# Last SSD group's output blocks and the layer norm behind them in token halves

## The chip, the cores and the metric

The kernel runs on one core of one Trainium2 chip. Its time is the device time of one launch in microseconds (us). Before the change it is 3307.63 us, the median of 3 runs (3304.9 to 3308.18).

## The reference

The program computes five layers on one sequence of 1024 tokens and width 1024, all in float32: an RG-LRU and latent-attention layer, a state space layer (SSD), and then a block of a feed-forward layer (FFN), a mixer and a second FFN. The change is in the seam between the SSD layer and the first FFN:

```
def _ssd_layer(x, w_in, conv_w, conv_b, dt_bias, a_log, d_skip, norm_w, w_out):
    ...
    y = _ssd_scan(xs, dt, a_neg, bm, cm) + d_skip.astype(jnp.float32)[:, None] * xs.astype(jnp.float32)
    y = y.reshape(bsz, seqlen, SSD_INNER) * jax.nn.silu(z.astype(jnp.float32))
    yg = y.reshape(bsz, seqlen, SSD_GROUPS, SSD_INNER // SSD_GROUPS)
    yg = yg * lax.rsqrt(jnp.mean(yg * yg, axis=-1, keepdims=True) + 1e-6)
    y = (yg.reshape(bsz, seqlen, SSD_INNER) * norm_w.astype(jnp.float32)).astype(x.dtype)
    return jnp.einsum('bse,ed->bsd', y, w_out)
...
            x = _layernorm(DN_ALPHA * x + y, ssd_ln_g[j], ssd_ln_b[j])
...
        h = rms_norm(x, ffn1_pre_g[l])
        x = x + 0.5 * rms_norm(swiglu(h, ffn1_w_in[l], ffn1_w_out[l]), ffn1_post_g[l])
```

There are four SSD groups of 512 channels. Each group is gated, normed by the root mean square over its 512 channels, and multiplied by its 512 rows of `w_out`.

## The kernel before

Activations lie transposed, features on the 128 partitions and tokens along the free axis: `ACC` is [128, 8 tiles, 1024 tokens]. A "token half" is 512 tokens, `half(0)` or `half(1)`, and h0 and h1 below. Each engine has a program of its own, written out in the order in which it runs, and semaphores join them. Nothing reorders them: an instruction that waits holds up all behind it on its engine.

A float32 product is made of three fast ones (fp32r). Weights `WS` and inputs are split into a high part (by ScalarE, `split_hi`, L333) and a low part (by VectorE, `split_lo`, L340), and TensorE adds high x high, high x low and low x high (`block_products`, L376). A block is 128 output features; in the SSD output projection it has 4 contraction tiles, so 12 products in one token half and 24 in both, and in the FFN 8 tiles, so 24 products in one half. Weight blocks alternate between two slots, and so do the PSUM banks `PS[0]` and `PS[1]`. Sums over features, which the norms want, are matmuls with `ONES` in plain float32; here each shows as two records in the trace.

The last SSD group (`g` = 3) runs so. The scan goes over 8 chunks of 128 tokens. In chunk 7 TensorE does the first two output blocks on h0 (`ssd_last_half`) between the chunk's first product and `ssd_outputs`. Their input `YLH`, `YLL` needs the gate's last block `z3`, its silu, the gating by VectorE (`ssd_last_gate`) and the split (`high`, `ssd_last_low`). Behind the scan come, on TensorE: 8 sums of squares (L1777), the first two blocks on h1, six blocks on both halves, 4 filler matmuls (`keep_busy`, L357), then the layer norm: 2 row sums (L1503) and 16 sums of squares (L1507). VectorE multiplies each block's PSUM by the group's root and adds it to `ACC` (`acc_vector`, L1461 and L1462), and adds rows up for the mean (L1472). The layer norm centres `ACC` (L1488), ScalarE squares it (L1511) and takes the root with Ln and Exp (L1516, L1517), VectorE scales (L1494), ScalarE adds the bias (L1521).

The first FFN begins with 8 blocks on h0 and 8 on h1 (j = 0 to 7 each; `ffn_tensor`). Its input is `ACC` again split (`pre_high` L2186, `pre_low` L2195) and squared for its own norm (L2190); GpSimd adds these squares up (`pre_sum`, L2203) for h0, TensorE for h1 (`head_row`, L2214). `pre_rows` (L2207) and `pre_rstd` (L2220, L2224) give the root that `ffn_hidden` (L2712 to L2721) needs before it can free a PSUM bank. The next two weight blocks are split in `ffn_gated` (L2635), behind the silu. After block 1 of h0 TensorE runs 15 filler matmuls.

Of the kernel before, what the change touches and what calls it, by code (L numbers as in the profile page):

```python
# [20 lines left out]
P = 128  # L21
# [123 lines left out]
def _build(nc, ctx, ins, out):  # L145
# [63 lines left out]
    YLH = at("YLH", 64, [P, 4, SEQ], F32R)  # L209
    YLL = at("YLL", 80, [P, 4, SEQ], F32R)  # L210
# [1243 lines left out]
    def acc_vector(dve, st, b0, turn, rooted=0):  # L1454

        for m in range(KT):
            b = b0 + m
            dve.wait_ge(BLOCK_DONE[b % 2], times(b))
            if rooted:
                dve.wait_ge(RSTD, rooted)  # L1460
                st.link(nc.vector.tensor_tensor(PS[b % 2][:], PS[b % 2][:], T[1][:], ALU.mult))  # L1461
            nc.vector.tensor_tensor(ACC[:, m], ACC[:, m], PS[b % 2][:], ALU.add).then_inc(PS_READ[b % 2], 1)  # L1462
            if m == KT - 1:
                row_sum(dve, st, b, m, turn)
            split_lo(dve, b + 2, cols=cols_of(b + 2))
            if 0 < m < KT - 1:
                row_sum(dve, st, b, m, turn)
# [30 lines left out]
    def ln_tensor(pe, turn, name):
        sq0 = NORM[name][1]
        keep_busy(PA, 4)  # L1500
        pe.wait_ge(LN_VECTOR, LN_TURN * turn + MSUM + 1)
        for h in range(2):
            nc.tensor.matmul(PB[:, half(h)], ONES[:], T[2][:, half(h)], start=True, stop=True).then_inc(MROW, 1)  # L1503
        for h in range(2):
            for k in range(KT):
                pe.wait_ge(SQ, sq0 + KT * h + k + 1)
                nc.tensor.matmul(PA[:, half(h)], ONES[:], SQB[:, k, half(h)], start=(k == 0), stop=(k == KT - 1)).then_inc(SUMMED, 1)  # L1507
# [387 lines left out]
    def ssd_last_scalar(act, st, g):  # L1895
# [19 lines left out]
        for k in range(4):  # L1915
            high(0, k)
# [1906 lines left out]
```

## Time and profile before

| | |
|---|---|
| median of 3 runs | 3307.63 us |
| profiled execution: its span, first to last instruction (the page gives no other time of it) | 3306.2 us |
| TensorE busy | 3189.7 us, 96% |
| VectorE busy | 2013.8 us, 61% |
| ScalarE busy | 1287.6 us, 39% |
| GpSimd busy | 356.9 us, 11% |
| mean granted TensorE clock | 0.990 |

Of the chain that ended last, 83% of the span is TensorE's. So a change counts where TensorE stands still or does what need not be done. The stage of the change lies at 1270 to 1430 us of the span. A timeline row reads: start, duration, engine, line, operation, output<-inputs, count, and in brackets how long the engine was idle before it and who ended that. Matmuls overlap, so a matmul's duration is longer than the distance from one start to the next.

### The profile page before, as it was taken

How to read it: one execution, taken by the hardware profiler on the slowest of the kernel's cores; microseconds unless marked ns; L12 is line 12 of the kernel's file. 1: busy time of each engine (PE TensorE's matmuls, PEld its weight loads, DVE VectorE, ACT ScalarE, POOL GpSimd, SP SyncE). 2: the span in 40 equal slices, each digit the busy share in tenths (PEclk: the TensorE clock that was granted, in tenths of full speed). 3: DMA queues.
4: the chain of work that ended last, by engine and by line, in shares of the span. 5: the costliest groups of instructions: out<-in, count | busy, mean ns of one | idle time of the engine just before them, and what ended most of it. 6: DMA issues, size and time to landing. Idle time of an engine off the chain costs nothing.

```text
span 3306.2 us, 40063 instructions
## 1 busy us (share of the span) xinstructions
PE 3189.7 (96%) x15986; PEld 2491.6 (75%) x15986; DVE 2013.8 (61%) x2760; ACT 1287.6 (39%) x1906; POOL 356.9 (11%) x421
## 2 busy tenths in 40 slices
PE   8999999999999998899999999998988899999999
PEld 7765577878787786578888888786666678888887
DVE  5544567664554645667777665586664877767334
ACT  2554435452525344643333223413525542323123
POOL 1011000110302011100000003140011200000012
PEclk9999999999999999899999999999999999999999
DMA  6220111222513132332223334423044432224234
GB/s 161 50 42 6 55 52 53 76 88 77 103 52 118 48 92 68 99 105 90 77 90 111 128 112 134 140 74 90 1 115 127 146 118 77 77 102 161 75 100 136
DMA packets 359543, 299.54 MB, mean 91 GB/s; under 512 B 55200, under 2 KB 320768, under 8 KB 358816
## 3 DMA queue, kind: packets, MB, share of 16 engines
q1 hardware_dynamic: 336496, 215.29, 22.3%
q0 software_dynamic: 22864, 81.69, 8.0%
q8 instruction: 128, 2.10, 0.3%
q14 instruction: 55, 0.45, 0.0%
HBM read 240.45 MB, written 52.95 MB: 89 GB/s over the span
## 4 chain that ended last, share of the span: by engine, by line
PE 83%; DVE 8%; ACT 4%; issue 3%; DMA 1%; SPq 0%; POOL 0%; DVEq 0%; ACTq 0%; POOLq 0%
PE PS L376 48%; PE PS L2529 13%; PE PA L2529 7%; PE PA L904 1%; PE PS L893 1%; PE PS L1100 1%; PE PB L916 1%; DVE WL L340 1%; PE PB L1840 1%; PE PS L1105 1%; PE PA L416 1%; PE PB L1179 1%; PE PB L1846 1%; PE PA L1822 1%; PE PS L1553 1%
## 5 line engine op out<-in xcount | busy, mean ns | idle before, releaser
L376 PE MATMUL PS<-XH,WH 128*128 128x512 f32 x1744 | 594.0, 405 | 25.7 <-DVE XL L2195 15.4
L333 ACT ACTIVATE WH<-WS 128x1024 fp32r<-128x1024 f32 (+1 forms) x251 | 242.3, 968 | 836.4 <-PE PS L376 811.5
L376 PE MATMUL PS<-XH,WL 128*128 128x512 f32 x1680 | 553.5, 391 | 0.0
L376 PE MATMUL PS<-XL,WH 128*128 128x512 f32 x1648 | 541.5, 391 | 0.0
L376 PEld LDWEIGHTS PS<-XH,WH 128*128 128x128 f32 x1744 | 326.0, 188 | 120.1 <-issue 21.4
L340 DVE TENSOR_TENSOR WL<-WS,WH 128x1024 fp32r<-128x1024 f32 (+1 forms) x251 | 283.0, 1128 | 155.2 <-ACT WH L333 141.4
L376 PEld LDWEIGHTS PS<-XH,WL 128*128 128x128 f32 x1680 | 316.4, 188 | 67.6
L376 PEld LDWEIGHTS PS<-XL,WH 128*128 128x128 f32 x1648 | 310.5, 188 | 68.0 <-issue 4.1
L376 PE MATMUL PS<-TQH,WH 128*128 128x512 f32 x448 | 160.1, 392 | 1.4 <-DVE WL L340 1.4
L376 PE MATMUL PS<-TQH,WL 128*128 128x512 f32 x448 | 158.8, 389 | 0.0
L376 PE MATMUL PS<-TQL,WH 128*128 128x512 f32 x448 | 158.7, 389 | 0.0
L2529 PE MATMUL PS<-XH,PH 128*128 128x512 f32 x360 | 140.2, 390 | 1.7 <-issue 1.7
L2529 PE MATMUL PS<-XH,PL 128*128 128x512 f32 x360 | 140.1, 389 | 0.0
L2529 PE MATMUL PS<-XL,PH 128*128 128x512 f32 x360 | 140.0, 389 | 0.0
L1953 ACT ACTIVATE DEC<-DEC,NCS 128x128 f32<-128x128 f32 x256 | 78.3, 388 | 99.1 <-POOL DEC L2069 99.0
L1974 DVE TENSOR_TENSOR DEC<-DEC,PB 128x1024 f32<-128x1024 f32 x32 | 39.1, 1221 | 125.3 <-ACT DEC L1953 103.5
L2529 PE MATMUL PS<-TQH,PH 128*128 128x512 f32 x288 | 112.5, 391 | 1.7 <-DVE U3S L2772 1.0
L2529 PE MATMUL PS<-TQH,PL 128*128 128x512 f32 x288 | 112.1, 389 | 0.0
L2529 PE MATMUL PS<-TQL,PH 128*128 128x512 f32 x288 | 112.0, 389 | 0.0
L2529 PE MATMUL PA<-TQH,PH 128*128 128x512 f32 x288 | 112.0, 389 | 0.0
L2529 PE MATMUL PA<-TQL,PH 128*128 128x512 f32 x288 | 112.0, 389 | 0.0
L2529 PE MATMUL PA<-TQH,PL 128*128 128x512 f32 x288 | 112.0, 389 | 0.0
(697 smaller groups left out, 6164.3 us busy)
## 6 DMA issues: line engine op xcount, KB each, us to landing
RAW<-in_ffn_w_in_dram SPq DMA_DIRECT2D x36, 1024.0 KB, 5.5
WS<-in_ffn_w_out_dram SPq DMA_DIRECT2D x48, 512.0 KB, 3.9
WS<-in_ssd_w_in_dram SPq DMA_DIRECT2D x40, 512.0 KB, 3.8
DEC<-ssd_decay_sums SPq DMA_DIRECT2D x32, 512.0 KB, 4.8
WS<-in_ffn_w_in_dram SPq DMA_DIRECT2D x32, 512.0 KB, 4.1
CDX<-ssd_decays SPq DMA_DIRECT2D x56, 256.0 KB, 3.7
TQF<-ffn_hidden POOLq DMA_DIRECT2D x14, 1024.0 KB, 8.3
x_residual<-ACC POOLq DMA_DIRECT2D x6, 2048.0 KB, 7.9
```

The lines of the kernel that those rows point to most:

```text
L333: nc.scalar.activation(WH[:, s, 0:cols], WS[:, s, 0:cols], ACT.Copy).then_inc(W_HI[s], 1)
L340: nc.vector.tensor_tensor(WL[:, s, 0:cols], WS[:, s, 0:cols], WH[:, s, 0:cols].bitcast(F32), ALU.subtract).then_inc(W_LO[s], 1)
L376: last = nc.tensor.matmul(PS[s][0:width, c], w[:, s, k * width:(k + 1) * width], x[:, k - x0, c], start=(k == 0 and j == 0), stop=(k == kt ...
L416: last = nc.tensor.matmul(PA[:, h * HALF:(h + 1) * HALF], ONES[:], bufs[k % 2][:, h * HALF:(h + 1) * HALF], start=(k == 0), stop=(k == kts ...
L893: last = nc.tensor.matmul(PS[s][:, a + c * P:a + (c + m) * P], self.queries(p, s)[:, qb * P:(qb + 1) * P], self.keys(p, s)[:, c * P:(c + m ...
L904: last = nc.tensor.transpose(PA[:, s * HALF + (kb - 4 * c) * P:s * HALF + (kb - 4 * c + 1) * P], self.probs(u, s)[:, kb * P:(kb + 1) * P], ...
L916: last = nc.tensor.matmul(PB[HD * s:HD * s + HD, HALF + (qb % 4) * P:HALF + (qb % 4 + 1) * P], self.values(p, s, kb), PT[u % 2][:, s, kb * ...
L1100: nc.tensor.matmul(PS[s][:, a + c * P:a + (c + m) * P], QT[t][rows, 0, q], KTT[t][rows, 0, c * P:(c + m) * P], start=True, stop=False)
L1105: last = nc.tensor.matmul(PS[s][:, a + c * P:a + (c + m) * P], QT[t][rows, 1, q], KTT[0][rows, 1, c * P:(c + m) * P], start=False, stop=True)
L1953: last = nc.scalar.activation(d, d, ACT.Exp, bias=NCS[:, c, k:k + 1])
L1974: v.tensor_tensor(DEC[n % 2][:], DEC[n % 2][:], PB[:, 0:P].unsqueeze(1).broadcast_to([P, HPG, P]), ALU.mult).then_inc(SMR, 1)
L2529: last = nc.tensor.matmul(bank, w[:, j, k * P:(k + 1) * P], x[:, k], start=(j in (A11, S2, S1) and k == 0 and t == 0), stop=(k == 3 and t ...
```

## The change

- The output weights of the last group are split once, into the free h1 halves of `XH` and `XL` (`out_high`, `out_low`), and serve both halves. The eight blocks run on h0 first and then on h1, each in half a bank (`out_bank`), so four products can stand before the first is read.
- The split of the first two weights, the gate's silu and the gated input come ahead of the decay of chunk 7 on ScalarE (`ssd_last_scalar`), and on VectorE ahead of that chunk's mixing. The third output weight's load stands later in SyncE's queue.
- The squares of the group's norm are added on GpSimd (`ssd_last_added`), and TensorE sums once for each half. Rows for the mean are added on GpSimd too (`ln2_row`).
- The layer norm of h0 runs beside the h1 output blocks, and that of h1 beside the FFN's h0 blocks (`ln2_beside_scalar`, `ln2_beside_vector`, `ln2_beside_tensor`). The FFN's squares of h1 are added on GpSimd as well. Both fillers are gone.

```diff
@@ ssd_sync
-                if c % 2 == 0:
+                if c % 2 == 0 and (c < TT - 2 or g < LAST):
                     ssd_load(sp, *after[c // 2 - 1])
@@ TensorE
+    def ssd_out_half(pe, h, m):
+        b = SSD_AT[LAST, "out", m]
+        s, n = b % 2, KT * h + m
+        if h == 0:
+            pe.wait_ge(W_LO[s], times(b))
+            if m < 2:
+                pe.wait_ge(PS_READ[s], times(b) - 1)
+        if 4 <= n < 12:
+            pe.wait_ge(OUT_FREE, OUT_FREE0 + n - 3)
+        if n >= 12:
+            pe.wait_ge(PS_READ[s], times(b - 4))
...
+    def ssd_last_out(pe):
         for m in range(2, KT):
-            block_products(pe, SSD_AT[g, "out", m], YLH, YLL, kt=4)
+            ssd_out_half(pe, 0, m)
+            if m == 2:
+                ssd_last_sum(pe, 0)
+            if m == 6:
+                ssd_last_sum(pe, 1)
+        for m in range(KT):
+            ssd_out_half(pe, 1, m)
+            if m == 0:
+                ln2_mean(pe, 0)
+            if m == 2:
+                ln2_squares(pe, 0)
...
-                    pe.wait_ge(RSTD, NORM["ln2"][0] + 2)
-                    keep_busy(PA, 15)
...
+    def ln2_beside_tensor(pe, j):
+        if j == 0:
+            ln2_mean(pe, 1)
+        if j == 2:
+            ln2_squares(pe, 1)
+        if j == 7:
+            pre_rows(pe, 0, 1)
@@ ScalarE
+        weights(0)
+        high(0, 0)
+        high(0, 1)
+        ssd_gate_silu(act, g, 3)
+        high(0, 2)
+        high(0, 3)
+        weights(1)
+        ssd_decay(act, g, TT - 1)
         for k in range(4):
             square(0, k)
+        weights(2)
+        weights(3)
+        nc.scalar.activation(EP[:, 8:9], EP[:, 0:1], ACT.Ln)
+        high(1, 0)
+        high(1, 1)
+        weights(4)
+        root(0)
...
+    def ln2_scalar(act, st):
         for k in range(KT):
+            ln2_square(act, 0, k)
+        nc.scalar.activation(EP[:, 10:11], EP[:, 0:1], ACT.Ln)
+        ln2_rstd(act, st, 0)
+        for k in range(KT):
+            ln2_bias(act, 0, k)
+            pre_high(act, 0, 0, k)
+        for k in range(KT):
+            pre_square(act, 0, 0, k)
+        nc.scalar.activation(EP[:, 11:12], EP[:, 0:1], ACT.Ln)
+        pre_rstd(act, st, 0, 0)
+        for k in range(KT):
+            ln2_square(act, 1, k)
+
+    def ln2_beside_scalar(act, st, f):
+        if f == 0:
+            ln2_rstd(act, st, 1)
+        if f == 1:
+            for k in range(KT):
+                ln2_bias(act, 1, k)
+                pre_high(act, 0, 1, k)
+        if f == 2:
+            for k in range(KT):
+                pre_square(act, 0, 1, k)
+        if f == 3:
+            pre_rstd(act, st, 0, 1)
@@ VectorE
+        for m in range(4, KT):
+            ssd_out_read(dve, st, 0, m)
+        ssd_out_read(dve, st, 1, 0)
+        ln2_center(dve, 0, range(KT))
+        for m in (1, 2):
+            ssd_out_read(dve, st, 1, m)
+        for b in (B_FFN1, B_FFN1 + 1):
+            split_lo(dve, b)
+        ssd_out_read(dve, st, 1, 3)
+        ln2_apply(dve, 0, range(3))
+        ssd_out_read(dve, st, 1, 4)
+        for k in range(KT):
+            pre_low(dve, 0, 0, k)
+            if k + 3 < KT:
+                ln2_apply(dve, 0, [k + 3])
+            if k < 3:
+                ssd_out_read(dve, st, 1, 5 + k)
...
+    def ln2_beside_vector(dve, f):
+        if f == 1:
+            ln2_apply(dve, 1, range(KT))
+        if f == 2:
+            for k in range(KT):
+                pre_low(dve, 0, 1, k)
@@ GpSimd
     def ln2_pool(pool):
+        ssd_last_added(pool, 0)
+        for m in range(1, 3):
+            ln2_row(pool, 0, m)
+        ssd_last_added(pool, 1)
+        for m in range(3, KT):
+            ln2_row(pool, 0, m)
+        for m in range(1, KT):
+            ln2_row(pool, 1, m)
+        for h in range(2):
+            for k in range(KT):
+                pre_sum(pool, 0, h, k)
+            pool.wait_ge(LNB, (3 + h) * KT)
+            spill_pool(pool, 0, h)
```

`ssd_out_read` is the pair of VectorE instructions that multiplies half a bank by the root and adds it to `ACC`; `OUT_FREE` and `PS_READ` count them.

Two places show how the order moves. ScalarE in the FFN's h0 blocks, from the root of the FFN's norm (Ln, Exp) on. `T_67` is the gate's silu, `WH` a weight split, `SQQ` and `T_69` the squares of the FFN's norm. Before:

```order
L2224 ACTIVATE T_69<-T_69 128x512
L1521 ACTIVATE ACC<-ACC,VT 128x512 x8
L2635 ACT_TABLE_LOAD
L2635 ACTIVATE T_67<-T_67 128x512
L333 ACTIVATE WH<-WS 128x1024 x2
L2186 ACTIVATE XH<-ACC,VT 128x512
L2190 ACTIVATE T_69<-ACC 128x512
L2186 ACTIVATE XH<-ACC,VT 128x512
L2190 ACTIVATE SQQ_191<-ACC 128x512
L2635 ACTIVATE T_67<-T_67 128x512
L333 ACTIVATE WH<-WS 128x1024 x2
```

The same place now, up to the second silu:

```order
L2340 ACTIVATE T_69<-T_69 128x512
L1488 ACTIVATE SQB<-ACC 128x512 x8
L2808 ACT_TABLE_LOAD
L2808 ACTIVATE T_67<-T_67 128x512
L333 ACTIVATE WH<-WS 128x1024 x2
L1498 ACT_TABLE_LOAD
L1498 ACTIVATE ZT<-PA,EP 128x512
L1499 ACT_TABLE_LOAD
L1499 ACTIVATE ZT<-ZT 128x512
L2808 ACT_TABLE_LOAD
L2808 ACTIVATE T_67<-T_67 128x512
L333 ACTIVATE WH<-WS 128x1024 x2
```

Where ScalarE had two splits and two squares between silus, it now has the layer norm's root; behind the second pair of `WH` come 8 pairs of bias (L1510) and high part (L2295), and behind the third 8 squares (L2306).

VectorE in the same blocks, third and fourth hidden tile (`T_67`, `T_68` from PSUM; `WL` the low part of a weight). Before, behind the fourth weight split of h0:

```order
L2195 SCALAR_TENSOR_TENSOR XL<-ACC,VT,XH 128x512 x4
L2712 TENSOR_TENSOR T_67<-PS,T_69 128x512
L340 TENSOR_TENSOR WL<-WS,WH 128x1024
L2718 TENSOR_TENSOR T_68<-PS,T_69 128x512
L2721 TENSOR_TENSOR T_68<-T_68,T_67 128x512
L340 TENSOR_TENSOR WL<-WS,WH 128x1024
L2195 SCALAR_TENSOR_TENSOR XL<-ACC,VT,XH 128x512 x2
```

Now:

```order
L1505 SCALAR_TENSOR_TENSOR ACC<-ACC,VT,ZT 128x512 x8
L2887 TENSOR_TENSOR T_67<-PS,T_69 128x512
L340 TENSOR_TENSOR WL<-WS,WH 128x1024
L2893 TENSOR_TENSOR T_68<-PS,T_69 128x512
L2896 TENSOR_TENSOR T_68<-T_68,T_67 128x512
L340 TENSOR_TENSOR WL<-WS,WH 128x1024
L2311 SCALAR_TENSOR_TENSOR XL<-ACC,VT,XH 128x512 x8
```

The low parts of h1, which were spread in twos and fours, stand in one run of 8 before the fourth hidden tile, and the layer norm's scaling of h1 in one run of 8 before the third.

## Rows read from the trace of the kernel before

**Rows 1.** TensorE's waits, 1225 to 1500 us: waiter <- releaser: total, times, longest
```profile
PE PS L376 <- DVE XL L2195: 7.9, 8, 2.2
PE PS L376 <- DVE YLL L2035: 7.6, 1, 7.6
```
**Rows 2.** Busy time by stretch (stretch, its length, engines, clock, DMA share, GB/s)
```profile
1269.91:1287.26 17.35, 9.75 (x56) 7.82 (x56) 7.56 (x11) 9.79 (x19) 1.15 (x2) 0.70 0.14 47
1287.26:1334.60 47.34, 45.84 (x187) 34.64 (x186) 34.58 (x36) 14.21 (x20) 0.00 (x0) 1.00 0.16 47
...
1356.00:1390.20 34.20, 25.60 (x80) 17.25 (x80) 20.51 (x23) 29.37 (x42) 11.83 (x9) 0.75 0.21 80
1390.20:1429.70 39.50, 39.49 (x159) 29.89 (x160) 18.65 (x23) 15.69 (x24) 0.00 (x0) 1.00 0.51 150
```
**Rows 3.** TensorE in order of time
```profile
1266.97 0.61 PE L376 MATMUL PS<-XH,WL 128*128 128x512 f32 x2
...
1277.51 0.77 PE L376 MATMUL PS<-YLH,WH 128*128 128x512 f32 x1 [7.61 <-DVE YLL L2035]
...
1282.29 0.39 PE L376 MATMUL PS<-YLH,WL 128*128 128x512 f32 x1
...
1285.37 1.09 PE L1840 MATMUL PB<-DEC,XTOK 128*64 128x128 f32 x16
...
1287.26 7.38 PE L1777 MATMUL PA<-T,ONES 128*128 128x512 f32 x16
...
1363.49 0.79 PE L376 MATMUL PS<-XH,WH 128*128 128x512 f32 x1 [2.23 <-DVE XL L2195]
...
1378.51 0.39 PE L376 MATMUL PS<-XL,WH 128*128 128x512 f32 x1
...
1382.39 6.63 PE L357 MATMUL PA<-ONES 128*128 128x256 f32 x30
```
**Rows 4.** ScalarE in order of time
```profile
1270.08 2.44 ACT L1953 ACTIVATE DEC<-DEC,NCS 128x128 f32<-128x128 f32 x8 [7.22 <-POOL DEC L2069]
1272.54 1.28 ACT L1877 ACT_TABLE_LOAD   x1
1273.84 1.02 ACT L1877 ACTIVATE ZT<-PS 128x1024 f32<-128x1024 f32 x1
...
1275.28 2.55 ACT L1902 ACTIVATE YLH<-ZT,VT 128x512 fp32r<-128x512 f32 x4
1277.73 2.18 ACT L1913 ACTIVATE T<-ZT 128x512 f32<-128x512 f32 x4
...
1355.46 0.71 ACT L1521 ACTIVATE ACC<-ACC,VT 128x512 f32<-128x512 f32 x1
1356.20 0.72 ACT L2186 ACTIVATE XH<-ACC,VT 128x512 fp32r<-128x512 f32 x1
1356.83 0.61 ACT L2190 ACTIVATE SQQ<-ACC 128x512 f32<-128x512 f32 x1
```
**Rows 5.** VectorE in order of time
```profile
1288.10 2.50 DVE L2030 TENSOR_TENSOR ZT<-ZT,XST 128x512 f32<-128x512 f32 x4
...
1357.62 1.78 DVE L1494 SCALAR_TENSOR_TENSOR ACC<-ACC,VT,T 128x512 f32<-128x512 f32 x1
1359.32 0.74 DVE L2195 SCALAR_TENSOR_TENSOR XL<-ACC,VT,XH 128x512 fp32r<-128x512 f32 x1
...
1390.07 0.68 DVE L2718 TENSOR_TENSOR T<-PS,T 128x512 f32<-128x512 f32 x1
1390.79 0.69 DVE L2721 TENSOR_TENSOR T<-T,T 128x512 f32<-128x512 f32 x1
1391.40 1.22 DVE L340 TENSOR_TENSOR WL<-WS,WH 128x1024 fp32r<-128x1024 f32 x1
```
**Rows 6.** GpSimd in order of time
```profile
1359.40 3.48 POOL L2203 TENSOR_TENSOR T<-T,SQQ 128x512 f32<-128x512 f32 x2 [0.56 <-ACT SQQ L2190]
...
1369.01 1.33 POOL L2203 TENSOR_TENSOR T<-T,SQQ 128x512 f32<-128x512 f32 x1 [4.44 <-ACT SQQ L2190]
```

More of the change, by code:

```diff
@@ L1452, in out1_scalar @@
             ln1_high(act, 1, k)
[L1454 to L1467, printed above, removed]
@@ L1498, in ln_tensor @@
[L1498 to L1507, printed above, removed]
@@ new lines, in _build, with ln2_row @@
+    ROWSUM = [ZT[:, h, LO_H] for h in range(2)]
+    LN2_ROOT = [ZT[:, 2 + h, LO_H] for h in range(2)]
+    def ln2_row(pool, h, m):
+        b = SSD_AT[LAST, "out", m]
+        if h == 0:
+            pool.wait_ge(OUT_FREE, OUT_FREE0 + m + 1)
+        else:
+            pool.wait_ge(PS_READ[b % 2], times(b))
+        if m > 1:
+            pool.wait_ge(LN_ROWS, LN_ROWS0 + 7 * h + m - 1)
+        c, d = half(h), ROWSUM[h]
+        nc.gpsimd.tensor_tensor(d, ACC[:, 0, c] if m == 1 else d, ACC[:, m, c], ALU.add).then_inc(LN_ROWS, 1)
@@ L1766, in ssd_tensor, with out_high @@
                                after=(lambda k: pe.wait_ge(SYGL, 4 * g + k + 1)) if m == 0 else None)
[L1768 to L1781 removed]
+    def out_high(m):
+        return XH[:, m, HI_H]
@@ new lines, in out_low, with gated, out_bank @@
+    def out_low(m):
+        return XL[:, m, HI_H]
+    def gated(h, k):
+        return (XH[:, k, LO_H], XL[:, k, LO_H]) if h == 0 else (YLH[:, k], YLL[:, k])
+    def out_bank(h, m):
+        return PS[SSD_AT[LAST, "out", m] % 2][:, half(m // 2 % 2)]
+    def ssd_out_half(pe, h, m):
+        b = SSD_AT[LAST, "out", m]
+        s, n = b % 2, KT * h + m
+        if h == 0:
+            pe.wait_ge(W_LO[s], times(b))
[5 more added lines that the diff above has]
+            pe.wait_ge(PS_READ[s], times(b - 4))
+        for k in range(4):
+            if m == 0:
+                pe.wait_ge(SYGL, 4 * LAST + 4 * h + k + 1)
+            hi, lo = gated(h, k)
+            w = slice(k * P, (k + 1) * P)
+            for j, (wt, x) in enumerate(((out_high(m), hi), (out_high(m), lo), (out_low(m), hi))):
+                last = nc.tensor.matmul(out_bank(h, m), wt[:, w], x, start=(k == 0 and j == 0), stop=(k == 3 and j == 2))
+        last.then_inc(BLOCK_DONE[s] if h == 0 else OUT_DONE, 1)
@@ L1783, in last_square @@
     def last_square(h, k):
-        return T[(2, 0, 1, 2)[2 * h + k // 2]][:, half(k % 2)]
+        return T[(2, 0, 1, 0)[2 * h + k // 2]][:, half(k % 2)]
+    LAST_ROOT = [T[2][:, half(h)] for h in range(2)]
     def ssd_in(pe, g, j, ks=None):
@@ L1870, in ssd_scalar @@
             ssd_skip(act, g, 3)
-            for c in range(TT):
+            for c in range(TT if ahead else TT - 2):
                 if c < TT - 1:
@@ new lines, in ssd_out_read @@
+    def ssd_out_read(dve, st, h, m):
+        b = SSD_AT[LAST, "out", m]
+        if h == 0:
+            dve.wait_ge(BLOCK_DONE[b % 2], times(b))
+        else:
+            dve.wait_ge(OUT_DONE, OUT_DONE0 + m + 1)
+        if m == 0:
+            dve.wait_ge(G_ROOT, G_ROOT0 + h + 1)
+        c, ps = half(h), out_bank(h, m)
+        st.link(nc.vector.tensor_tensor(ps, ps, LAST_ROOT[h], ALU.mult))
+        nc.vector.tensor_tensor(ACC[:, m, c], ACC[:, m, c], ps, ALU.add).then_inc(OUT_FREE if h == 0 else PS_READ[b % 2], 1)
@@ L2815, in ffn_vector @@
         u = 2 * turn
+        if u == 0:
+            ln2_center(dve, 1, range(KT))
         for h in range(2):
```

264 lines of the change are left out of this document (151 added, 113 removed).

## Prediction

> **What bounds the kernel now.** TensorE is 96% busy, so I first read its waits around the change. Two groups stand out: 7.6 us in one piece for the gated input of the last group, and 7.9 us in eight pieces for the low parts of the FFN's input [rows 1]. Then the busy time by stretch. Between the scan's last chunk (its end I call A, 1287.3) and the end of the output blocks (1334.6) TensorE is full. From 1356.0 to 1390.2 it is busy 25.6 of 34.2 us with the clock at 0.75 of full speed, and from 1390.2 (J, the FFN's third block) to 1429.7 (H, the first block of h1) it is full again [rows 2]. What is busy there is not all useful: the 15 fillers take 6.6 us and end where the splits of the third block end [rows 3]. So 55.6 us lie between the last output block and J, in which the layer norm, two FFN blocks and a root run one behind the other, and TensorE waits for ScalarE and VectorE. Last, the rows of those engines give the price of each instruction.
>
> **Prices.** Start to start: a product 0.227 us (24 in 5.45), a float32 sum 0.86 (8 matmuls, 16 records, in 7.38 with the last one's end [rows 3]). ScalarE: copy or high part 0.62, square 0.52 (4 in 2.18, the last ends late), decay of a chunk 2.44, table load 1.28, silu of a gate block 1.0, bias and high part 1.37 together (0.74 because the second needs the first, and 0.63) [rows 4]. VectorE: 0.61 on half a tile (4 in 2.50), multiply by the root and add 1.33 (0.72 to the dependent one, then 0.61), weight split low 1.2, and 0.67 for a scaling or a low part, which shows 0.74, but 1.78 when GpSimd adds at that time: 1.04 lost [rows 5]. GpSimd: an add 1.33, 1.74 when VectorE works against it [rows 6].
>
> **Work alone.** From A to H TensorE needs 142.4 us now. Afterwards it has 14 half blocks of 12 products (38.2), 22 float32 sums for 2 + 1 + 8 + 1 + 8 + 2 (19.0) and 8 FFN blocks (43.7): 100.9. Six sums of the group's norm, seven of the FFN's, the fillers and all waits are gone from that sum: 41.5 us. I don't expect them, because the other engines' chains set the pace. I follow these piece by piece.
>
> **Up to A.** The gate's block ends at 1267.6 [rows 3]. ScalarE then does two weight splits, four high halves and the silu (6 x 0.62 + 1.0 = 4.7), with 0.6 of waiting for VectorE's gating, loads a table (1.28) and makes the decay (2.44); VectorE's mixing is 1.2 and the outputs on TensorE 1.9 (1285.4 to 1287.3 [rows 3]): 1279.8. The first two half blocks fit under that (5.5 us from about 1270). I add 0.7 for a slow clock: A = 1280.5, 6.8 us sooner. The load of the third weight, moved behind the first split, takes about 3 us from 1269 (an estimate from its size against 512 KB blocks that land in 4 us on the page) and is wanted at 1280: 7 us of cover. Without it the excess would be paid in full.
>
> **A to the end of the output blocks.** VectorE has, before the first read, four gates (2.5), two low halves, three weight parts, and a root from ScalarE that ends at A + 7.7. The first read ends at A + 9.1, and TensorE, which may be four halves ahead, waits 2.6 us. It waits 0.9 for a weight part behind that, and 2.9 for the second trio of adds on GpSimd, which stands behind two row sums and ends at A + 21.0. Nine half blocks (24.6), 11 sums (9.5) and 6.5 of waits bring it to the last sum of squares of h0, S = A + 40.6 = 1321.1. Five half blocks more: 1334.7. That is where it ends today. The gain of the first part is spent, though eight sums of squares are done.
>
> **To J.** Behind S the root takes 2.9 us. VectorE then has 5 reads (6.7), 8 scalings (5.4), 5 low parts (3.4), and a row sum on GpSimd after each read, which blocks the next instruction: 5 x 1.04 = 5.2. The last scaling ends at S + 23.6, its high part at S + 25.1. Only now come the squares of the FFN's norm, which today run beside: 1.1 for two, then 7 adds in a row on GpSimd, 9.2. Sum over rows and hop 1.1, root 2.6, the 8 squares of h1 that stand ahead of the silu 4.2, table and silu 1.8, high and low part of the next weight 2.3: J = S + 47.5 = 1368.6. TensorE has 12.6 us of work in these 34 and no filler. J is 21.6 us sooner.
>
> **J to H.** Block, with 2.0 for the slow clock after such a gap (4.8 us at half speed [rows 3] would cost 2.2), 7.5; eight sums 6.9; root 2.8; silu with table 1.8; two high parts 2.1. VectorE splits the second weight until J + 23.8 and then scales; ScalarE's 8 pairs of bias and high part run from 24.5 to 35.5 (11.0) with the third pair of weights queued behind them. TensorE waits 6 us for block 6. Silu and splits take it to 38.1. Then 7 adds (1.04 of lock each, 7.3) meet 6.9 us of VectorE work with two SBUF inputs, of which the 8 low parts are 5.4: J + 53.4. Only behind them VectorE frees block 6 (0.7), then silu 0.55, high part 1.05, low part 1.2: H = J + 56.9 = 1425.5. Today this stretch is 39.5. So 17.4 of the 21.6 are given back. The wait ahead of H (TensorE is ready by J + 50) costs another 2.4 in clock: 1427.9, 1.8 us sooner than now. Behind H the order is the old one, and I move it all by 1.8.
>
> The profiled execution's span is 3306.2, 1.4 below the median; from the span the sum gives 3304.4, from the median **3305.8 us**. I take the latter.
>
> **A rule against it.** The lock shows in the 1.78 against 0.74 [rows 5] and the 1.74 against 1.33 [rows 6]. The Trainium skill (SBUF — State Buffer, section "SBUF: two separate sides") says that a VectorE instruction with two SBUF inputs and a GpSimd instruction that reads SBUF shut each other out for the whole instruction. By that the 12 blocked instructions would lose 1.33 instead of 1.04 each, 3.5 us more: 3309.3. The row is this kernel's, so the sum keeps it. That adds on half banks with one PSUM input go free is my assumption, since the row of GpSimd's adds has no such neighbour.
>
> **Rivals.**
> - *The chains give way.* If GpSimd's adds fall in VectorE's pauses, the 5.2, the 7.3 and the 2.9 go: H 15.4 earlier, **3290.4**. For it: the squares come one by one. Against it: rows 5 and 6 show adds and scalings alternate without a gap. If even ScalarE's run of 8 pairs hid, TensorE's work alone would hold: 6.8 + 41.5 = 48.3, **3259.3**.
> - *The clock.* Today the clock came back 4.8 us after the 7.6 us wait (1277.5 to 1282.3), but only 14.9 us after the stretch of small waits (1363.5 to 1378.5) [rows 3]. Without fillers two waits of 7 us or so stand ahead of J and H. Should each take 14.9 us, half of it lost, 7.0 each against the 2.0 and 2.4 that I count: 9.6 more, **3315.4**, slower. It decides as soon as both returns need over 14 us; at 4.8 it is my forecast. The rows show one of each.
> - *The first part isn't earned.* If chunk 7's decay, now behind the silu and six copies, comes so late that A stays at 1287.3: 6.8 more, 3312.6. Against it: 7 us between 1267.6 and 1277.5 are idle in both engines.
>
> **How the numbers follow.** A difference of 0.2% (6.6 us) is about what a measurement tells from none. Forecast 40% (3299 to 3313; nearly all of it within 0.2%), chains give way 32%, work alone 5%, clock 17%, first part 6%. That makes faster 0.38, same 0.36, slower 0.26. The range takes in the first rival with some of what lies beyond it, and the clock: 3285 to 3318. The unknowns that carry it are the lock (down 15.4) and the clock (up 9.6).
>
> **What would show it.** Right: J some 20 us sooner than now and H near 1426; waits on TensorE for the low part of blocks 6 and 8 of the FFN's head of about 6 us each; VectorE's low parts of h1 at 1.7 instead of 0.74; output blocks that end near 1335; the clock under 1 before J. Wrong: H before 1415 or after 1436; TensorE full between J and H; low parts at 0.74, which would take the lock out of the sum; or a clock that stays low for over 10 us behind J.

## The result

| | before | changed |
|---|---|---|
| median | 3307.03 us (20 runs, 3303.96 to 3311.28) | 3313.23 us (20 runs, 3307.05 to 3316.59) |
| ratio, 95% interval | | 1.0015 (1.0009 to 1.0022) |
| a second set, on one chip | 3308.5 (33 runs) | 3312.81 (11 runs), ratio 1.0015 (1.0006 to 1.0024) |
| span of the profiled execution | 3306.2 | 3312.4 |
| TensorE busy, mean granted clock | 3189.7, 0.990 | 3179.8, 0.986 |
| GpSimd busy | 356.9 | 396.8 |

By the ratio the change costs 5 us (0.15%; the medians lie 6.2 apart), where I forecast a gain of 1.8 us (3305.8). That is under the 0.2% I had called "same" and inside the range, but the interval of the ratio is clear of 1: the sign is wrong. A small part lies outside the span: the launch takes 1.6 to 1.7 us more than its span in every run of the kernel before whose span is on record, and 1.6 to 2.8 (mean 2.2) in the 20 runs of the changed one. Why is open.

**TensorE's waits afterwards**, 1225 to 1500 us of the changed kernel (waiter <- releaser: total, times, longest). The 7.6 us for the gated input [rows 1] are gone, and 19.2 and 6.8 us have come:

```profile
PE PS L376 <- DVE WL L340: 19.2, 5, 6.1
PE PB L2323 <- POOL T L2319: 6.8, 2, 6.4
...
PE PA L1784 <- POOL T L2447: 2.4, 1, 2.4
PE PS L376 <- DVE XL L2311: 2.0, 2, 1.4
PE PS L1779 <- DVE ACC L2103: 1.7, 1, 1.7
```

**Busy time by stretch of the changed kernel** (stretch, length, then PE, PEld, DVE, ACT, POOL busy, granted clock, DMA share, GB/s): up to A, A to the end of the output blocks, to J, J to H, the first block of h1. They answer to [rows 2]:

```profile
1272.00:1281.40 9.40, 7.51 (x53) 5.43 (x53) 7.36 (x11) 8.54 (x19) 2.20 (x2) 1.00 0.36 109
1281.40:1335.70 54.30, 48.52 (x191) 35.20 (x190) 45.00 (x60) 31.23 (x45) 23.49 (x17) 1.00 0.20 58
1335.70:1371.50 35.80, 19.04 (x55) 12.57 (x53) 19.05 (x25) 22.77 (x34) 14.22 (x11) 0.77 0.16 59
1371.50:1428.40 56.90, 45.10 (x162) 32.81 (x162) 30.70 (x32) 28.22 (x39) 12.36 (x8) 0.89 0.30 96
1428.40:1437.40 9.00, 8.94 (x28) 7.18 (x29) 3.04 (x5) 4.88 (x5) 0.00 (x0) 0.70 0.73 214
```

The first part is won (the clock is 1.00 up to A, where it was 0.70), TensorE is busy 19.0 of 35.8 us before J and 45.1 of 56.9 behind it, and the clock is below full speed in each of the last three stretches. Before, it was 1.00 from J on.

To compare executions I need a start and an end that the change does not touch. I take VectorE's add into PREV of the last chunk as zero and its first copy into TQF as the end, first the kernel before, then the changed one:

```profile
1273.77 0.68 DVE L2051 TENSOR_TENSOR PREV<-PREV,PA 128x512 f32<-128x512 f32 x1
1443.60 2.28 DVE L2580 TENSOR_TENSOR TQF<-ACC 128x2048 f32<-128x2048 f32 x1
```

```profile
1275.09 0.68 DVE L2160 TENSOR_TENSOR PREV<-PREV,PA 128x512 f32<-128x512 f32 x1
1444.63 2.29 DVE L2753 TENSOR_TENSOR TQF<-ACC 128x2048 f32<-128x2048 f32 x1
```

This stretch is 169.8 us before and 169.5 after. In the first pair of traces, then, the edited region costs nothing; 1.3 us of the later end are there ahead of it and 4.5 us come behind it, from TQF to the last VectorE instruction. So further traces of both kernels come first. All times "from PREV" below are differences of such rows.

### The profile page after: what moved, and what is told of

It is laid out like the page before. It is cut to its first block, busy times and chain, and to the rows that moved or that the text cites. A ratio compares the mean times of both kernels' runs of the same rounds, so it can differ in the third digit from the quotient of the medians.

```text
span 3312.4 us, 39982 instructions
## 1 busy us (share of the span) xinstructions
PE 3179.8 (96%) x15922; PEld 2488.4 (75%) x15922; DVE 2017.6 (61%) x2769; ACT 1295.3 (39%) x1916; POOL 396.8 (12%) x448
## 4 chain that ended last, share of the span: by engine, by line
PE 82%; DVE 9%; ACT 4%; issue 3%; DMA 1%; POOL 1%; SPq 0%; DVEq 0%; ACTq 0%; POOLq 0%
PE PS L376 46%; PE PS L2704 13%; PE PA L2704 7%; PE PA L904 1%; PE PS L893 1%; DVE WL L340 1%; PE PS L1100 1%; PE PB L916 1%; PE PB L1859 1%; DVE XL L2311 1%; PE PS L1105 1%; PE PA L416 1%; PE PA L1841 1%; PE PB L1179 1%; PE PB L1865 1%
## 5 line engine op out<-in xcount | busy, mean ns | idle before, releaser
L376 PE MATMUL PS<-TQL,WH 128*128 128x512 f32 x448 | 158.7, 389 | 0.0
```

The costliest lines, as they stand in the source:

```text
L376: last = nc.tensor.matmul(PS[s][0:width, c], w[:, s, k * width:(k + 1) * width], x[:, k - x0, c], start=(k == 0 and j == 0), stop=(k == kt ...
```

## The experiments

Two theories. **Chains**: what the change gained is given back because GpSimd's adds, their hold on VectorE, and the bundles of ScalarE work that stand in one piece set J and H. **Clock**: TensorE now waits bare, without fillers, and pays for each return at 1.2 GHz. And a question: is the rest behind the stretch chance?

| run | stretch | clock 1270 to 1440 | median | ratio to before (95%) |
|---|---|---|---|---|
| before, four traces | 169.8, 168.9, 168.6, 169.2 | 0.92 to 0.93 | | |
| changed, four traces | 169.5, 169.6, 172.0, 169.7 | 0.88 to 0.90 | 3312.81 | 1.0015 (1.0006 to 1.0024) |
| e3 fillers in all four waits | 164.8 | 0.97 | 3306.15 | 0.9999 (0.9990 to 1.0008) |
| e13 fillers in the first two | 166.5 | 0.94 | 3309.96 | 1.0010 (1.0001 to 1.0019) |
| e14 fillers in the last two | 169.8 | 0.91 | 3308.69 | 1.0006 (0.9997 to 1.0015) |
| e8 before, its fillers removed | 173.2 | 0.89 | 3313.03 | 1.0016 (1.0008 to 1.0025) |
| e4 squares summed on TensorE | 167.6 | 0.93 | 3309.24 | 1.0003 (0.9994 to 1.0012) |
| e5 the same with eight buffers | 167.6 | 0.93 | 3308.73 | 1.0001 (0.9992 to 1.0010) |
| e6 squares of h1 ahead of the root | 166.5 | 0.91 | 3308.47 | 1.0004 (0.9995 to 1.0013) |
| e9 low parts early | 165.7 | 0.90 | 3303.39 | 0.9989 (0.9980 to 0.9998) |
| e7 = e5 + e6 + fillers | 161.9 | 0.96 | 3299.01 | 0.9982 (0.9974 to 0.9991) |
| e10 = e9 + e6 + fillers | 159.8 | 0.97 | 3301.39 | 0.9980 (0.9971 to 0.9989) |

The runs belong to four sets on four chips, in which the kernel before had medians of 3308.5 (e1 to e4), 3307.9 (e5 to e8), 3307.59 (e9, e10) and 3306.34 (e13, e14). So ratios are compared across sets, not medians. Beside e3 and e4 the changed kernel ran 11 times in the same set, and both are faster than it by more than the scatter (in the mean 6.2 us, +/- 2.3, and 3.9 us, +/- 1.7). Of the others, the intervals of e7, e9 and e10 lie wholly below the changed kernel's; those of e5, e6, e13 and e14 overlap it, and what these gain is read from their traces.

Each trace is one execution. In e9, e14 and the third trace of the changed kernel block 0, which waits for the first root, is read 1.4 us later (89.5 us from PREV instead of 88.1). Its origin shows in windows of that third trace: behind the 2.4 us wait for GpSimd's trio, TensorE's clock falls, which in the other three traces of the changed kernel it does not. The same fall is in e7's trace. I call this the late root and compare like with like.

```profile
1300.00:1305.00 5.00, 2.60 (x9) 1.46 (x8) 4.38 (x7) 0.81 (x2) 4.78 (x4) 0.93 0.51 151
1305.00:1310.00 5.00, 5.00 (x18) 4.00 (x17) 1.39 (x2) 3.81 (x4) 3.18 (x3) 0.73 0.00 0
```

### e1, e2, e11, e12, e15, e16: both kernels again

No edit. The changed kernel:

> The changed kernel once more, for its time beside the others on one chip and for a second trace. In the first pair of traces the changed stretch as a whole (VectorE's square-sum add into TQF, 1443.60 before, 1444.63 after) is 1.0 us late, of which 1.2 us was there by 22 us of the span; another 4.3 us come between 2374 and 2440 us of the span, a stage that was not edited. Theory A (the changed stretch returns exactly what it gains, and the rest of the 5 us lies in the later stage): the offset at TQF less the offset at the start is 0 to 1 us again, and the later stage is again 3 us or more late. Theory B (the later stage is chance of one execution, and the changed stretch costs the 5 us in most executions): the stretch is 3 to 5 us late and the later stage on time.

> A third trace of the changed kernel: stretch 169.6 within 0.5 us; behind it 1862 to 1863 if the stage behind differs with the change, anything from 1858 to 1864 if it is chance.

> A fourth trace of the changed kernel. Stretch so far 169.5, 169.6, 172.0; behind it 1862.8, 1862.8, 1860.7. Below 1860 behind it: chance; 1861 to 1863 again: it goes with the change.

The kernel before:

> The kernel before once more, ratio 1.000 within 0.1%. For a second trace of it: theory B expects the stage between 2374 and 2440 us to vary by some 4 us between two executions of the same kernel, theory A expects it to stay within 1 us of its first length.

> A third trace of the kernel before, for the stage behind the changed stretch (from VectorE's first TQF copy to the end: 1858.3 and 1860.7 us in two traces of it, 1862.8 twice in the changed kernel, 1861.4 to 1863.6 in the experiments). If the stage behind really differs with the change: 1858 to 1861 again. If it is chance: a value about 1862 is as likely.

> A fourth trace of the kernel before. Stretch so far 169.8, 168.9, 168.6; stage behind it 1858.3, 1860.7, 1858.0. A stage behind of 1862 or more here would say that the 3 us by which the changed kernel's traces are longer behind the stretch come of chance in the executions; 1858 to 1860 that they go with the change.

e2's ratio to the other runs of the same kernel is 0.9997 (0.9988 to 1.0006). The 4.3 us between 2374 and 2440 us of the first pair, which e1's first theory expected again, did not come again there: e1's trace loses as much, but further back. e12's stretch (172.0) missed the 169.6 expected, by the late root. Over four traces each the stretch is 169.1 before and 170.2 after: +1.1. The time ahead of it (start to PREV) is 1273.8, 1275.0, 1271.9, 1273.9 before and 1275.1, 1274.8, 1275.9, 1274.0 after: +1.3, with overlap, and in code that is the same up to the last chunks. The nine experiments on the changed kernel have that code too and take 1271.9 to 1275.6, 1273.6 in the mean like the kernel before, so I take this 1.3 for chance. Behind it, to the last VectorE instruction, 1858.3, 1860.7, 1858.0, 1860.6 before and 1862.8, 1862.8, 1860.7, 1863.4 after: +3.0. e11 (1858.0) fell to "differs with the change", e12 (1860.7) to "chance", e15 (1860.6) lies between the two outcomes I had named; e16 (1863.4) said "goes with the change". The experiments, whose code behind the stretch is the same too, give 1861.4 to 1863.6 and once 1866.6 (e10).

What varies there can be named: the granted clock. Two windows where the first pair of traces parts, of before and then of the changed kernel (columns as above):

```profile
2300.00:2400.00 100.00, 91.10 (x821) 62.23 (x823) 67.45 (x150) 55.05 (x130) 0.00 (x0) 1.00 0.03 10
2400.00:2450.00 50.00, 43.36 (x477) 33.31 (x473) 33.11 (x43) 11.51 (x16) 7.95 (x9) 1.00 0.35 106
```

```profile
2300.00:2400.00 100.00, 91.14 (x808) 61.80 (x807) 67.91 (x152) 54.90 (x131) 0.00 (x0) 1.00 0.02 5
2400.00:2450.00 50.00, 43.49 (x411) 35.15 (x409) 28.72 (x36) 11.73 (x16) 7.95 (x9) 0.90 0.38 115
```

The same work with the same short waits runs at 1.00 in one execution and at 0.90 in the other (411 matmuls recorded in 50 us instead of 477). A second place is 2530 to 2620: 1.00 in the first trace of before, 0.96 in its fourth. e1's trace, of the changed kernel too, has the two the other way round:

```profile
2400.00:2450.00 50.00, 43.53 (x483) 33.82 (x481) 32.87 (x42) 11.48 (x16) 7.95 (x9) 1.00 0.37 113
2530.00:2620.00 90.00, 79.04 (x322) 61.35 (x321) 57.37 (x60) 41.85 (x57) 36.81 (x28) 0.96 0.51 155
```

Behind TQF all 18 traces hold the same 1767 VectorE instructions. Lined up one by one they stay within 0.6 us of each other for the first 600 us, part between there and 1280 us (some 2050 to 2720 us of the span), and from there on keep their distances within 0.4 us. From 1450 to 2050 and from 2720 to 3290 us the clock is 1.00 in every one of them. So the time behind the stretch differs by the granted clock in that one stage, and a part of the 3.0 us comes and goes between executions of one kernel. But the four traces of before are the four shortest of the 18 (one of the changed kernel ties with them at 1860.7), and even e8, which is the kernel before less some fillers, takes 1863.5. That speaks against chance alone, and against the changed order as the cause. I have not shown what makes the other kernels meet the low clock there more often. It stays open.

### e3: fillers in TensorE's four waits

```
+ FILL, FILL_ROWS = {(0, 2): 12, (0, 6): 12, (1, 0): 8}, 12
+ if turn == 0 and (h, j) in FILL:
+     keep_busy(PA, FILL[h, j])            # ahead of blocks 2, 6 and 8
  if turn == 0 and h == 0 and j == 1:
      block_products(pe, b, XH, XL, h=h, ks=range(0, 2))
+     keep_busy(PA, FILL_ROWS)             # ahead of the row sum of h0
      pre_rows(pe, 0)
```

> The changed kernel with filler matmuls (the same helper as before had at two places) in the four waits of TensorE: 12 ahead of the row sum of the first token half, 12 ahead of block 2 of the FFN head, 12 ahead of block 6, 8 ahead of the first block of the second half. One is 0.43 us at full clock. Clock theory (what was given back is TensorE's work at the lower granted clock behind its waits: blocks 2, 6 and 8 took 7.8, some 5.6 and 8.3 us where 5.5 is their length at full clock): the granted clock is 1.00 through 1350 to 1440, block 2 ends 2.0 us earlier and block 8 2.5 us, row sum 1.0 us: 4 to 5.5 us faster than the change, some 3308.5 us. Chain theory (GpSimd's sums and their hold on VectorE set the ends): block 6 is waited for by VectorE anyway, so at most 2.5 us behind block 8 and 2 us behind block 2, and the waits themselves stay as long: 6.4, 6.1, 5.8 and 4.2 us less the fillers.

3306.15 us, 6.7 us under the changed kernel of the same set (its ratio to before is 0.9999, the change's 1.0015). VectorE's reads tell where, from PREV, against the first trace of the changed kernel: the read of block 0, which waits for the root, 87.1 (88.1); block 2 101.3 (104.2); block 6 146.9 (149.8); block 8 157.0 (161.7). So 1.0 us at the row sum, 2.0 at block 2, nothing at block 6, 1.8 at block 8: 4.8 us. The row sum of h0 in the changed kernel, then in e3:

```profile
1358.41 2.08 PE L2323 MATMUL PB<-T,ONES 128*128 128x512 f32 x2 [6.35 <-POOL T L2319]
```

```profile
1356.98 1.13 PE L2323 MATMUL PB<-T,ONES 128*128 128x512 f32 x2 [1.03 <-POOL T L2319]
```

Block 2 of TensorE in the changed kernel starts after 6.06 us of waiting at 0.43 us a product, and at 1375.9 falls to 0.23.

```profile
1371.52 0.80 PE L376 MATMUL PS<-XH,WH 128*128 128x512 f32 x1 [6.06 <-DVE WL L340]
1372.11 0.63 PE L376 MATMUL PS<-XL,WH 128*128 128x512 f32 x1
1372.54 0.63 PE L376 MATMUL PS<-XH,WL 128*128 128x512 f32 x1
...
1375.89 0.39 PE L376 MATMUL PS<-XL,WH 128*128 128x512 f32 x1
1376.12 0.40 PE L376 MATMUL PS<-XH,WL 128*128 128x512 f32 x1
```

The clock theory holds with its own number for the stretch (4 to 5.5 us). The time fell by more, and the rest isn't in the stretch.

### e13, e14: the first two fillers, the last two

```
e13: FILL, FILL_ROWS = {(0, 2): 12}, 12
e14: FILL, FILL_ROWS = {(0, 6): 12, (1, 0): 8}, 0
```

> The changed kernel with e3's fillers at the first two waits alone (12 ahead of the first half's row sum, 12 ahead of block 2); the waits ahead of blocks 6 and 8 stay bare. e3 took the stretch from 170.4 (mean of three traces of the change) to 164.8. If each return costs what its block loses (row sum and rest of block 1: 1 to 1.4 us, block 2: 2.0 us; block 8: 2.5 us, block 6 nothing because VectorE is later), this one gives 167.0 to 167.5, about 3309.5 us.

> The changed kernel with e3's fillers at the last two waits alone (12 ahead of block 6, 8 ahead of block 8). By the same count the stretch gives 170.4 - 2.5 = 168 (block 6's return is hidden behind VectorE's low parts), about 3310.5 us. If block 6's return counts too: 166.

e13: block 8 is read at 158.7 from PREV (161.7), -3.0; 3309.96 us, as expected. e14 has the late root: against the changed kernel's trace with the late root the reads are equal up to block 6 (151.84 and 151.85), and block 8 is at 161.9 (164.2), -2.2: also as expected (2.5). Its stretch of 169.8 alone would have said that nothing was won. Its time, 3308.69, is better than that of e13, by less than the intervals hold. In time neither is clear of the changed kernel; what is shown of the two halves is in the reads.

### e8: the kernel before without its fillers

```
- keep_busy(PA, 4)      # ahead of the layer norm's row sum
- keep_busy(PA, 15)     # in the FFN head, behind the root
```

> The kernel before without its two sets of filler matmuls (4 ahead of the layer norm's row sum, 15 behind the first root of the FFN head). Clock theory: one more return at the lower granted clock, +1.5 to +4 us (3310 to 3312), with the sum of low-clock time in 1270 to 1440 us up from 24-27 us. If the change lost nothing by leaving them out: within 1 us of before.

3313.03 us: +0.16% (5.1 us on the median of its set), as much as the whole change and more than the 1.5 to 4 us expected. Block 0's read is 1.2 us later from PREV (108.6 against 107.4), block 2's 3.4 (125.6 against 122.2), and all that follows. The clock in 1270 to 1440 falls from 0.92 to 0.89. The rows are of TensorE in this kernel: the layer norm's row sums take 3.78 us, where the kernel before has 1.98 for them, and block 2 starts slow after 7.72 us.

```profile
1337.88 3.78 PE L1502 MATMUL PB<-T,ONES 128*128 128x512 f32 x4 [3.90 <-DVE T L1472]
...
1390.41 0.76 PE L376 MATMUL PS<-XH,WH 128*128 128x512 f32 x1 [7.72 <-issue]
```

So the two sets of fillers, 6.6 us of which [rows 3] I had called "not all useful", were together worth 5 us in the kernel before, and the change had dropped both.

### e4: the squares summed on TensorE

```
- pool: pre_sum(pool, 0, h, k) for 7 adds in each half
+ pe:   head_row(pe, 0, k, h): 8 matmuls with ONES into PB, h0 inside block 1, h1 behind block 6
+ act:  squares to RPRE's half and SQQ[1], SQQ[0] in turn (three buffers)
```

> The changed kernel with the 2 times 7 adds of squares off GpSimd: TensorE adds the 8 squares of each token half in PSUM with the matrix of ones, as the kernel before does for its second half; three buffers for the squares. Chain theory: the squares of the first half follow each other at 0.57 us from 1347.4 and the root starts near 1352.8 where it started at 1360.5, so block 2 starts near 1363.8 in place of 1371.5 (-7.7); in the second half VectorE's 8 low parts take 0.74 us each in place of 1.4 to 1.77 (11.6 us become 5.9), so the second half starts some 5.5 us earlier still: 13 us in all, 3300 us, faster than both kernels. Clock theory alone: the same waits stand in other places, at most 3 us.

3309.24 us: -3.6, not -13. At J hardly anything is won: block 2 is read at 103.5 from PREV in place of 104.2, where 7.7 us were expected, because ScalarE's squares now wait 4.1 us for TensorE's sums. In the second half the hold on VectorE was real. The eight low parts of h1 in the changed kernel, beside GpSimd's adds, and then in e4 without them:

```profile
1413.35 11.59 DVE L2311 SCALAR_TENSOR_TENSOR XL<-ACC,VT,XH 128x512 fp32r<-128x512 f32 x8
```

```profile
1410.17 5.38 DVE L2309 SCALAR_TENSOR_TENSOR XL<-ACC,VT,XH 128x512 fp32r<-128x512 f32 x8
```

Block 6 is read at 141.9 from PREV in place of 149.8. But block 8 is read at 159.8 (161.7), because ScalarE in e4 stands in a wait that I had not priced: its fourth square needs a buffer that TensorE frees behind block 6, and block 8's weights are queued behind the squares.

```profile
1416.46 0.63 ACT L2304 ACTIVATE T<-ACC 128x512 f32<-128x512 f32 x1 [7.42 <-PE PB L2328]
```

### e5: the same with eight buffers

```
- dst = head_square(k) ...                 # three buffers
+ dst = SQB[:, k, c] if u == 0 else ...    # eight, free by then
```

> As e4, but the squares of the two token halves go to the eight free slots of SQB in place of three buffers, so ScalarE no longer waits for TensorE's rows (in e4: 4.1 us ahead of the root of the first half, 7.4 us ahead of block 8's weights). Chain theory: the 8 squares of the first half take 4.3 us in a row, the root starts some 3 us earlier than in e4; the second half's splits no longer wait, TensorE is held only by its own rows and blocks, so H is some 3 us earlier again: stretch from VectorE's last PREV add to TQF 167.6 (e4) to some 162, about 3303.5 us. If ScalarE's waits in e4 were no limit, 167.6 stays.

3308.73, stretch 167.6 as in e4: the 162 was missed, and "167.6 stays" came. ScalarE's squares now run in one piece and it waits later, for the sums themselves. They are float32, two records of 0.43 us each, and TensorE is behind:

```profile
1349.80 7.03 PE L2328 MATMUL PB<-SQB,ONES 128*128 128x512 f32 x16
...
1407.05 0.80 PE L376 MATMUL PS<-XH,WH 128*128 128x512 f32 x1 [5.77 <-DVE WL L340]
1414.61 7.03 PE L2328 MATMUL PB<-SQB,ONES 128*128 128x512 f32 x16
```

ScalarE waits 5.9 us for the first set. In the second half TensorE runs block 6, 7.0 us of sums, and block 7 without a pause, and block 8 stands behind them. Seven adds on GpSimd take 9.8 us, eight sums on TensorE 7.0: the exchange gains 3 us at best.

### e6: the squares of h1 ahead of the first root

```
- pre_rstd(act, st, 0, 0)
- for k in range(KT): ln2_square(act, 1, k)
+ for k in range(KT): ln2_square(act, 1, k)
+ pre_rstd(act, st, 0, 0)
```

> The changed kernel, with one thing moved: ScalarE's 8 squares of the second half's layer norm (4.25 us, between the root of the first half and the silu of blocks 0 and 1) stand ahead of that root, where ScalarE waits for GpSimd's sums anyway. Chain theory: block 2's silu, high and low part and so J come 4.2 us earlier (1371.5 to 1367.3), and as J to H is a chain of its own the whole stretch from 169.6 to 165.4: 3308.8 us. If the end of the stretch is set by something else (the second half's root, TensorE at its lower clock), under 1.5 us.

3308.47 us (3308.8 expected). From PREV, block 1 is read at 93.4 (96.3), block 2 at 100.9 (104.2), block 8 at 158.7 (161.7): -3.0 instead of the -4.2 expected, since the root now waits for the last square and ends 1.3 us later:

```profile
1354.87 4.25 ACT L1488 ACTIVATE SQB<-ACC 128x512 f32<-128x512 f32 x8
1359.02 0.67 ACT L2336 ACTIVATE T<-PB,EP 128x512 f32<-128x512 f32 x1
```

What block 2 gains, block 8 keeps: behind J the chain has its own length, as the chain theory has it.

### e9: the low parts early

```
  if f == 1:
      ln2_apply(dve, 1, range(KT))
+     for k in range(6): pre_low(dve, 0, 1, k)
  if f == 2:
-     for k in range(KT): pre_low(dve, 0, 1, k)
+     for k in range(6, KT): pre_low(dve, 0, 1, k)
```

> The changed kernel, with six of VectorE's eight low parts of the second half moved ahead of its read of block 4 (they follow ScalarE's high parts, ready from 1396), so that only two of them run beside GpSimd's seven adds. If the row of eight low parts beside the adds (11.6 us, 1413.35 to 1424.9, 1.45 us each) sets the start of the second half: VectorE reads block 6 as soon as TensorE has it (near 1415.5 in place of 1424.86), block 8's weights are split by 1419, TensorE runs blocks 6, 7 and 8 without a wait and H comes near 1422.5 in place of 1428.4: stretch from the last PREV add to TQF 169.6 to some 164, -5 to -6 us, 3307.5 us. If the root of the second half (behind the adds, row sum ready at 1423) takes its place: -1 to -2 us.

3303.39: faster than before (0.9989, interval below 1), and the largest gain of a single edit. By the ratios it is 8.6 us on the changed kernel, where 5 to 6 were expected; the trace shows 6.3 of it in the stretch (165.7 against 172.0 with the late root). Against the changed kernel's trace with the late root, block 6 is read at 144.7 from PREV in place of 151.9, block 8 at 156.6 in place of 164.2. Two low parts still meet the adds and pay (1.74 us each), six take 0.66 in a pause that VectorE had anyway:

```profile
1401.45 3.39 DVE L2311 SCALAR_TENSOR_TENSOR XL<-ACC,VT,XH 128x512 fp32r<-128x512 f32 x5
1405.31 0.75 DVE L2311 SCALAR_TENSOR_TENSOR XL<-ACC,VT,XH 128x512 fp32r<-128x512 f32 x1 [0.46 <-ACT XH L2295]
...
1414.19 3.47 DVE L2311 SCALAR_TENSOR_TENSOR XL<-ACC,VT,XH 128x512 fp32r<-128x512 f32 x2
```

### e7 and e10: together

```
e7:  e5 + e6 + FILL {(0, 2): 10, (0, 6): 12}
e10: e9 + e6 + FILL {(0, 2): 4, (0, 6): 12}, FILL_ROWS 12
```

> e5 and e6 together, and fillers in the two waits that stay long (10 ahead of block 2, 12 ahead of block 6). If the three causes (GpSimd's sums, squares in the way of the silu, granted clock behind the waits) add up: stretch 169.6 - 7.6 (e5) - 3.7 (less than in e6, as the root now waits for squares) - 2.5 (two blocks at full clock) = 155.8 or about 3299 us, 0.25% faster than before. If TensorE becomes the bound behind block 6 (its rows of squares and block 7 follow block 6 without a wait), some 3 us of it are lost: 3302.

> e9 and e6 together (low parts early, squares of the second half ahead of the first root), the sums on GpSimd as in the change, with fillers in three waits (12 ahead of the first half's row sum, 4 ahead of block 2, 12 ahead of block 6). If the effects add: 169.6 - 5.5 (e9) - 3.1 (e6) - 4.8 (e3, of which some 1.5 goes as block 8 has no wait left) = 157.7 or less, 3297 us, 2 us under e7 as TensorE's two times 7 us of rows of squares are gone. If e7's end was set by the same thing, 162 and 3299.

Both beat both kernels: 3299.01 (0.9982) and 3301.39 (0.9980), by the ratios some 6 us against before and 11 against the change. In e10's trace block 8 is read at 150.9 from PREV, where it was 162.0 before and 161.7 in the changed kernel; e7 reaches 154.1. e10's shorter stretch does not show in its time: its trace is the one with 1866.6 us behind, and the two ratios agree. Which is better isn't settled. The effects did not simply add: the stretches expected were 155.8 (e7) and 157.7 (e10), those measured 161.9 and 159.8. That e7's median is still the 3299 expected is luck in part. Its profiled execution took 3305.86; three of its 12 runs, this one among them, took 3305.9 to 3311.0 at a mean clock of 0.988 to 0.990, and the other nine 3296.7 to 3301.8 at 0.992 to 0.993. The profiled executions of e9 and e10 too are the slowest of their 11 runs.

## Why the prediction was wrong

By its own steps, the changed kernel's first trace against it, from PREV where a mark is given:

- **Up to A.** Right: 6.3 us, forecast 6.7, before 13.5. The gain of 6.8 is there in full, so the rival by which the first part isn't earned is out.
- **A to S, end of the output blocks.** Right: A to S 40.7 (40.6), end of the output blocks 60.6 (60.9; before 60.8). The waits are those named: 1.7 for the first read (2.6), 1.3 for weight parts (0.9), 2.4 for the second trio of adds (2.9). "The gain of the first part is spent" holds.
- **To J.** S to the last high part 25.3 (25.1). From there to J 24.1, forecast 22.4: the step is 1.7 short. The seven adds take 9.8 (9.2), because ScalarE and GpSimd hand two buffers to and fro, and the row sum, after 6.4 us of waiting, runs at the lower clock (1358.4 to 1360.5), which costs 1.0 by e3. ScalarE's and GpSimd's rows:

```profile
1351.34 0.63 ACT L2306 ACTIVATE SQQ<-ACC 128x512 f32<-128x512 f32 x1 [0.80 <-POOL T L2319]
1352.76 0.63 ACT L2306 ACTIVATE SQQ<-ACC 128x512 f32<-128x512 f32 x1 [0.79 <-POOL T L2319]
```

```profile
1348.58 9.77 POOL L2319 TENSOR_TENSOR T<-T,SQQ 128x512 f32<-128x512 f32 x7 [4.55 <-ACT SQQ L2306]
```

- **J to H.** Right to the tenth: 56.9 us, the pairs of bias and high part from J + 24.6 to 35.6 (24.5 to 35.5), the last low part at J + 53.4 (53.4), TensorE's wait for block 6 5.8 (6). The recorded terms for the last low part (38.1, 7.3 and 6.9) add up to 52.3 and not 53.4; the trace has the first add at J + 39.2, so the figure holds where its sum doesn't show it. That the order of the chain decides, and not the adds alone, e4, e6 and e9 show.
- **The lock.** Right: a row-sum add on GpSimd makes the next scaling 1.76 to 1.78 again [rows 5], and eight low parts beside seven adds take 11.6 instead of 5.4, 6.2 more. The weight split just ahead of them, whose row follows, takes 2.30 instead of 1.22, 1.1 more. That makes the 7.3 I counted, and the rival by which the adds fall in VectorE's pauses is out. By the rule of the Trainium skill (SBUF — State Buffer, section "SBUF: two separate sides"), with a whole add's 1.33 lost to each of seven, it would have been 9.3, an estimate. The trace bears out the exclusion, not its full price. My assumption that VectorE's adds with one PSUM input are free of it held too: they take 0.69 beside GpSimd's row sums.

```profile
1411.13 2.30 DVE L340 TENSOR_TENSOR WL<-WS,WH 128x1024 fp32r<-128x1024 f32 x1
```

- **The clock.** Wrong in size and number. The two returns I priced (2.0 and 2.4) cost 2.0 and 1.8 by e3, the second of them inside block 8 and not ahead of H. I had no price for a return at the row sum (1.0), and no term for what the removed fillers had been holding up. I weighed the fillers as TensorE work that goes and only the first of the following blocks as slow. e8 prices them: 5 us in the kernel before. The rival called "the clock" (each return 14.9 us) is not what happened either: block 2 is slow for 4.0 us (1371.5 to 1375.5) and block 8 for 5.4 (1428.5 to 1433.9). There are more returns, not ones of 14.9 us. The granted clock over 1270 to 1440 is 0.88 to 0.90 against 0.92 to 0.93.
- **"Behind H the order is the old one, and I move it all by 1.8."** This is the step that failed, together with the row sum's return in "To J", which I had put at nothing. In the first pair of traces the stretch moved by -0.3 us instead of -1.8, and the 1.5 between are J's: 0.6 in the adds, 1.0 in the clock at the row sum. From PREV, J is 20.0 us sooner (21.6 forecast) and H 2.6, but block 8 runs slow and is read only 0.3 sooner than before. Over four traces each the stretch moved by +1.1; of the difference to -0.3, 0.6 is the one trace with the late root and 0.7 is that the first trace of before was the longest of its four. Behind the stretch the same instructions took 3.0 us longer, and there the clock differs; ahead of it 1.3, chance as far as the traces tell. e3 and e8 show that fillers in this stretch move the time by more (6.7 and 5.1) than the stretch itself (5.4 and 4.1). Why the part behind the stretch is longer is open.

So the mechanism of the stretch was forecast well: nearly all that I had named as signs of being right is in the trace, the 20 us at J, the output blocks' end near 1335, low parts at up to 1.7 us, waits of 5.8 and 4.2 us ahead of blocks 6 and 8. What they couldn't tell is the sign of a balance of 1.8 us out of a give and take of 20, which one unpriced microsecond at the row sum and a few at the clock behind the stretch turned round.

## What to carry to other kernels

Before an edit removes filler work or opens a new wait on TensorE, price each return from a wait at the slow product rate (here 0.43 us a product instead of 0.23, 1 to 2 us lost each) and look for every one of them, not for the two largest. When work is cut into halves to start early, look at what is then put in one piece on the side engines: here eight squares in front of a silu and eight low parts beside seven GpSimd adds kept the halving from paying, and moving them (a few lines of order each) shortened the stretch by 3 and 6 us (in time some 4 and 9 by the ratios, the first within its interval). And compare unchanged marks in several traces before looking for a cause inside the edit.

## What was new about the hardware

- The same unchanged stage of one kernel ran at a granted clock of 1.00 or 0.90 to 0.96 in different executions (2400 to 2450 and 2530 to 2620 us), worth 2 to 4 us each time.
- Behind the same wait of 2.4 us, with the same instructions before it, the clock fell in four of 14 traces (the third of the changed kernel, e9, e14 and e7; 0.66 to 0.76 over 5 us) and in the other ten it did not. It cost 1.4 us where the rest of the order is the same.
- A weight split and eight low parts on VectorE (two SBUF inputs each) that met GpSimd's seven adds lost 7.3 us in all, 1.04 for each add; VectorE's adds with one PSUM input lost nothing.
- A float32 sum over the partitions costs TensorE 0.86 us for 512 columns, in two records, and eight of them 7.0 us; seven adds on GpSimd of the same width take 9.8 us. Neither is a cheap place.
